# A depthwise convolution shared out between three engines: GpSimd takes one channel tile of eight, TensorE four instead of five

## What is computed

```python
def conformer_conv(h, n_seg, w_pw1, b_pw1, w_dw, b_dw, ln_g, ln_b, w_pw2, b_pw2):
    B, L, D = h.shape
    u = h @ w_pw1 + b_pw1
    a, gate = jnp.split(u, 2, axis=-1)
    u = a * jax.nn.sigmoid(gate)
    u = dwconv(u.reshape(B * n_seg, L // n_seg, D), w_dw).reshape(B, L, D) + b_dw
    u = jax.nn.silu(layer_norm(u, ln_g, ln_b))
    return u @ w_pw2 + b_pw2
```

## Time and profile before

| | |
|---|---|
| median of 3 runs | 2293.07 us (2291.17 to 2293.07) |
| span of the profiled execution | 2286.9 us |
| TensorE, matmuls | 2214.6 us busy, 97% of the span |
| VectorE | 985.8 us, 43% |
| ScalarE | 393.5 us, 17% |
| GpSimd | 67.6 us, 3% |
| chain that ended last, by engine | TensorE 66%, issue 22%, DMA 7%, VectorE 3%, ScalarE 1% |

### The profile page before, as it was taken

One profiled execution on the slowest core, in us unless ns is written; L12 is line 12 of the kernel. 1 busy time (PEld: TensorE's weight loads), 2 busy tenths in 40 slices (PEclk: granted clock), 3 DMA queues, 4 the chain that ended last, 5 costly groups with the idle time before them and its releaser, 6 DMA issues.

```text
span 2286.9 us, 24807 instructions
## 1 busy us (share of the span) xinstructions
PE 2214.6 (97%) x10134; PEld 1284.9 (56%) x10134; DVE 985.8 (43%) x1358; ACT 393.5 (17%) x748; POOL 67.6 (3%) x84
## 2 busy tenths in 40 slices
PE   7999999999999999999899999999999899999998
PEld 3343488888885556765544444445885544444443
DVE  2883297788845651861322222115541322222222
ACT  3214222012123210750200000002000200000000
POOL 1100100000020000001000000000000000000000
PEclk9999999999999999999899999999999899999999
DMA  9316244677541111021699999998211399999996
GB/s 349 144 42 232 99 147 147 227 260 279 190 166 46 37 37 68 22 107 69 249 423 428 428 429 428 429 428 326 74 74 74 143 424 429 428 429 428 430 428 275
DMA packets 106458, 564.55 MB, mean 247 GB/s; under 512 B 8584, under 2 KB 17422, under 8 KB 78734
## 3 DMA queue, kind: packets, MB, share of 16 engines
q1 hardware_dynamic: 105952, 563.35, 61.3%
q10 hardware_dynamic: 430, 0.13, 0.0%
HBM read 561.36 MB, written 2.10 MB: 246 GB/s over the span
## 4 chain that ended last, share of the span: by engine, by line
PE 66%; issue 22%; DMA 7%; DVE 3%; ACT 1%; POOL 0%; DVEq 0%; SPq 0%; ACTq 0%; POOLq 0%
PE psum L1503 20%; PE psum L1257 15%; PE psum L1926 8%; PE psum L1912 4%; DMA ring<-in_moe_w_down_dram 3%; PE psum L1698 3%; PE psum L2005 2%; PE psum L1819 2%; PE psum L1962 2%; DMA ring<-in_mlp_w_dram 2%; PE psum L1450 2%; PE psum L1750 1%; PE psum L1777 1%; PE psum L1399 1%; DMA ring<-in_moe_w_up_dram 1%
## 5 line engine op out<-in xcount | busy, mean ns | idle before, releaser
L1926 PE MATMUL psum<-ring,arena 128*64 128x512 f32 x2048 | 444.5, 593 | 4.9 <-DMA ring<-in_moe_w_up_dram 4.9
L1926 PEld LDWEIGHTS psum<-ring,arena 128*64 128x64 f32 x2048 | 145.0, 137 | 301.2 <-issue 287.6
L1257 PE MATMUL psum<-hT,ring 128*128 128x512 f32 x608 | 267.4, 597 | 3.8 <-ACT hT L852 3.8
L1912 PE MATMUL psum<-ring,arena 128*64 128x512 f32 x768 | 224.5, 594 | 1.9 <-DMA ring<-in_moe_w_down_dram 1.9
L2653 DVE TENSOR_TENSOR arena<-psum,arena 128x512 f32<-128x512 f32 x32 | 33.9, 1059 | 409.9 <-PE psum L1926 409.9
L1257 PEld LDWEIGHTS psum<-hT,ring 128*128 128x128 f32 x608 | 116.0, 192 | 150.1 <-issue 143.4
L1503 PE MATMUL psum<-ring 128*128 128x256 f32 x640 | 142.9, 380 | 3.7 <-DVE rstd L2358 3.7
L1503 PE MATMUL psum<-hT,ring 128*128 128x256 f32 x608 | 138.8, 385 | 0.8 <-ACT hT L846 0.8
L1503 PEld LDWEIGHTS psum<-ring 128*128 128x128 f32 x640 | 121.0, 190 | 23.5 <-issue 7.3
L1962 PEld LDWEIGHTS psum<-arena 128*128 128x128 f32 x1024 | 120.8, 198 | 14.0 <-issue 14.0
L1503 PEld LDWEIGHTS psum<-hT,ring 128*128 128x128 f32 x608 | 117.1, 193 | 18.4 <-issue 2.2
(11 more groups left out here) (349 smaller groups left out, 2480.4 us busy)
## 6 DMA issues: line engine op xcount, KB each, us to landing
ring<-in_moe_w_gate_dram SPq DMA_DIRECT2D x64, 2048.0 KB, 19.1
ring<-in_moe_w_up_dram SPq DMA_DIRECT2D x64, 2048.0 KB, 16.2
ring<-in_moe_w_down_dram SPq DMA_DIRECT2D x44, 2048.0 KB, 19.6
ring<-in_ada_w_dram SPq DMA_DIRECT2D x24, 2048.0 KB, 8.7
ring<-in_mlp_w_dram SPq DMA_DIRECT2D x16, 2048.0 KB, 8.5
hT<-in_moe_w_down_dram SPq DMA_DIRECT2D x16, 2048.0 KB, 14.2
ring<-in_w_mod_dram SPq DMA_DIRECT2D x12, 2048.0 KB, 12.9
ring<-in_conv_w_in_dram SPq DMA_DIRECT2D x6, 2048.0 KB, 19.3
```

Of the source, the lines that this page charges most:

```text
L1257: ins = pe.matmul(bank[:, 0:width], w[:, k, col:col + P], src(k), start=start and k == 0, stop=stop and k == kts - 1)
L1912: ins = pe.matmul(psum[64 * e:64 * e + 64, bank + nh, :], src[:, 4 * h + k, 64 * e:64 * e + 64], w[:, k, nh * N:(nh + 1) * N], start=h == ...
L1926: ins = pe.matmul(psum[64 * nh:64 * nh + 64, bank + e, :], src[:, 4 * h + k, 64 * e:64 * e + 64], w[:, k, nh * N:(nh + 1) * N], start=h == ...
```

## The change

GpSimd convolves channel tile 1. VectorE convolves tiles 0, 2 and 4, TensorE tiles 3, 5, 6 and 7. [...] Its padded input `upad_pool` lies in the place of a constant that is loaded later. It does this after the first two tap matrices and before the last two. The orders on TensorE and ScalarE are written out anew; the means are summed in the order 0, 2, 1, 3, 4, 5, 6, 7. There is a 13th tap transfer. VectorE waits for its previous own tile to be complete before it writes `upad` again.

```diff
-N_TAPS = 12
-PE_CONV = (0, 2, 4, 6, 7)
-DVE_CONV = (1, 3, 5)
+N_TAPS = 13
+PE_CONV = (3, 5, 6, 7)
+DVE_CONV = (0, 2, 4)
+POOL_CONV = (1,)
...
-        if j % 2:
-            T_CV[j - 1] = tiles(["act"])
-    T_CV[DT - 1] = tiles(["act"])
+        if j == 5:
+            T_CV[3] = tiles(["act"])
+    for j in (5, 6, 7):
+        T_CV[j] = tiles(["act"])
...
+        upad_pool = carve(K, KCOL["cos"][0], SEGS, UPAD)
+        tap_u = carve(rms, 0, SEGS, SEG)
...
-                for m, j in enumerate(DVE_CONV):
-                    dst = vec_rows[0:TAPS, 5, :] if m == 2 else vec_rows[48 + TAPS * m:48 + TAPS * (m + 1), 2, :]
+                for m, j in enumerate(DVE_CONV + POOL_CONV):
+                    dst = vec_rows[TAPS * (m - 2):TAPS * (m - 1), 5, :] if m >= 2 else vec_rows[48 + TAPS * m:48 + TAPS * (m + 1), 2, :]
                     rows(sp, dst, A["conv_w_dw"][0][:, j * P:(j + 1) * P], "taps_in")
...
-            for m, j in enumerate(PE_CONV):
+
+            def spread_taps(m):
+
+                j = PE_CONV[m]
                 if m >= 2:
                     pool.wait_ge(S["tile_done"], T_CV[PE_CONV[m - 2]] + 1)
...
+            def pool_conv(m):
+
+                j = POOL_CONV[m]
+                pool.wait_ge(*emptied(T_PW1[j])(1))
+                link(pool.tensor_tensor(upad_pool[:, :, PAD:PAD + SEG],
+                                        glu_a[:, j % 2, :].rearrange("p (s w) -> p s w", s=SEGS),
+                                        glu_s[:, j % 2, :].rearrange("p (s w) -> p s w", s=SEGS), ALU.mult))
+                acc = cv[:, j, :].rearrange("p (s w) -> p s w", s=SEGS)
+                for k in range(TAPS):
+                    at = COL[f"w_own{len(DVE_CONV) + m}"] + k
+                    w, u = vecT[:, at:at + 1], upad_pool[:, :, k:k + SEG]
+                    if k == 0:
+                        ins = pool.tensor_scalar(acc, u, w, vecT[:, COL["b_dw"] + j:COL["b_dw"] + j + 1], ALU.mult,
+                                                 ALU.add).then_inc(S["u_pool"], 1)
+                        pool.wait_ge(S["u_pool"], m + 1)
+                    else:
+                        link(pool.tensor_scalar(tap_u, u, w, None, ALU.mult))
+                        ins = pool.tensor_tensor(acc, acc, tap_u, ALU.add)
+                        if k < TAPS - 1:
+                            link(ins)
+                ins.then_inc(S["conv_pool"], 1)
+
+            link(pool.memset(upad_pool[:, :, 0:PAD], 0.0))
+            link(pool.memset(upad_pool[:, :, PAD + SEG:UPAD], 0.0))
+            spread_taps(0)
+            spread_taps(1)
+            pool_conv(0)
+            spread_taps(2)
+            spread_taps(3)
...
-            for m in range(4):
-                pw1(2 * m)
-                spread(m)
-                pw1(2 * m + 1)
-                conv_out(2 * m)
-                if m == 3:
-                    spread(4)
+            for j in range(5):
+                pw1(j)
+            spread(0)
+            pw1(5)
+            conv_out(3)
+            pw1(6)
+            spread(1)
+            spread(2)
+            pw1(7)
+            conv_out(5)
+            spread(3)
+            conv_out(6)
...
-            for m in range(4):
-                pw1(2 * m)
-                if m == 0:
-                    pe.wait_ge(S["taps_in"], 16 * N_TAPS)
-                    pe.wait_ge(S["tap_pad"], 1)
-                    turn_tile(T_TAPS, [(vec_rows[0:VEC_ROWS[g], g, :], VEC_ROWS[g]) for g in range(2, 6)])
-                if m == 2:
-                    pe.wait_ge(S["rms_ready"], 1)
-                if m >= 2:
-                    conv_mean(2 * m - 3)
-                pw1(2 * m + 1)
-                conv(2 * m)
-                if m == 3:
-                    mod_gemv(1)
-                if m:
-                    conv_mean(2 * m - 2)
+            pw1(0)
+            pe.wait_ge(S["taps_in"], 16 * N_TAPS)
+            pe.wait_ge(S["tap_pad"], 1)
+            turn_tile(T_TAPS, [(vec_rows[0:VEC_ROWS[g], g, :], VEC_ROWS[g]) for g in range(2, 6)])
+            pw1(1)
+            pw1(2)
+            pw1(3)
+            pe.wait_ge(S["rms_ready"], 1)
+            conv_mean(0)
+            pw1(4)
+            pw1(5)
+            conv_mean(2)
+            conv(3)
+            pw1(6)
+            pw1(7)
+            conv_mean(1)
+            conv(5)
+            conv_mean(3)
+            conv(6)
+            conv_mean(4)
+            mod_gemv(1)
             conv_mean(5)
             conv(7)
...
                 m = DVE_CONV.index(j)
+                if m:
+                    dve.wait_ge(S["conv_done"], m)
                 dve.wait_ge(*emptied(T_PW1[j])(1))
...
             for j in range(DT):
                 if j in PE_CONV:
                     glu(j)
-                else:
+                elif j in DVE_CONV:
                     own_conv(j)
```

More of the change, by code:

```diff
@@ L64 @@
     ("b_mod2", 48), ("w_own0", TAPS), ("w_own1", TAPS), ("to_next_block", 18),
-    ("w_dw", ROUNDS * 32), ("w_own2", TAPS),
+    ("w_dw", ROUNDS * 32), ("w_own2", TAPS), ("w_own3", TAPS),
 ):
@@ L68 @@
     _at += _w
-VEC_ROWS = [128, 123, 48 + 2 * TAPS, 128, 128, TAPS]
+VEC_ROWS = [128, 123, 48 + 2 * TAPS, 128, 128, 2 * TAPS]
 KCOL = {}
@@ L279, in block_kernel @@
         K = sb("K", [P, KW])
-        vecT = sb("vecT", [P, 5 * P + TAPS])
+        vecT = sb("vecT", [P, 5 * P + 2 * TAPS])
         cpad = sb("cpad", [P, DT, 32])
@@ L425, in block_kernel @@
             "n_ms", "n_inv", "n_wide", "half_scaled", "half_ready", "late_sq",
-            "u_base", "u_ready", "u_spread", "u_own", "conv_done", "mean_done", "mean_sb", "centered",
+            "u_base", "u_ready", "u_spread", "u_own", "u_pool", "conv_done", "conv_pool", "mean_done", "mean_sb", "centered",
             "x_pw2", "gains", "hid_ready", "mlp_wsum", "mlp_wsum4", "mlp_tsum", "mlp_part", "mlp_m1", "mlp_read",
@@ L885, in pw1 @@
                         act.wait_ge(S["u_ready"], PE_CONV.index(j - 2) + 1)
-                    elif j >= 2:
+                    elif j - 2 in DVE_CONV:
                         act.wait_ge(S["u_own"], DVE_CONV.index(j - 2) + 1)
+                    elif j - 2 in POOL_CONV:
+                        act.wait_ge(S["u_pool"], POOL_CONV.index(j - 2) + 1)
                     col = COL["b_pw1"] + (8 if m == 0 else 0) + j
@@ L1457, in conv_mean @@
                     pe.wait_ge(*emptied(T_CV[j])(0))
+                elif j in POOL_CONV:
+                    pe.wait_ge(S["conv_pool"], POOL_CONV.index(j) + 1)
                 else:
```

## The result

The changed kernel takes 2308.44 us (median of 4 runs, 2306.99 to 2311.59), the kernel before 2292.12 us (4 runs) beside it: +16.3 us, ratio 1.0082, 95% interval 1.0069 to 1.0096. The forecast was +26.3 us, in a range of +11 to +43. The profiled execution has a span of 2305.8 us, 18.9 us longer than before, and the stage accounts for it: TensorE begins the sums after the mean 17.95 us later.

What follows compares the result with a forecast made beforehand. TensorE was taken to bound the stage; +30.7 us (late) +2.6 (clock) -7.0 (removed convolution) = +26.3 us, on the profiled 2286.9 us and the 6.2 us to the median: 2319.4 us. Range +11 to +43 us.

Steps and rivals of the forecast that it cites:

- removed convolution: One of five tile convolutions on TensorE taken out of the stage: -7.0 us if nothing waits.
- Price of a sum to a step: Time a GpSimd sum adds to a linked VectorE step while GpSimd's tile runs: 0.95 us.
- Price of a tensor_scalar: Time a GpSimd tensor_scalar adds to a VectorE step: 0.50 us taken, between nothing or 0.36 and 0.95.
- The pace: While GpSimd's tile runs, each VectorE step loses 0.725 us; a multiply-add goes every 1.51 us instead of 0.787.
- three signs of being wrong: Multiply-adds at 0.8 us beside GpSimd, multiply-adds alternating 1.7 and 0.75, or a wait on GpSimd's own tile.
- Late by 30.7: TensorE starts tile 3's convolution at 156.7 us instead of 126.0, after waiting for VectorE's tile 2 and replicas: +30.7 us.
- The clock: After its wait TensorE runs at the lower clock, near 0.5 for 5 us: +2.6 us, between 0 and 2.6.
- forecast's own lower bound: Low end for the forecast's own case, +20 to +42 us, 2313 to 2335 us.
- rival A: GpSimd's tensor_scalar operations hold nobody on VectorE: 14 us fewer, +12, 2305 us; chance 0.12.
- rival B: Faster: VectorE's slack takes all the holding, so the 7.0 us show, 2286 us; chance 0.05.
- Rival C: GpSimd's tensor_scalar is dearer than its sum, 1.5 us with a hold of 1.3: 22 more, 2342 us; chance 0.10.
- Rival D: Looser turns, VectorE getting two steps in between now and then: a loss of 0 to 12 us; chance 0.05.

Runs made afterwards that it cites:

- run without taps: Changed kernel with GpSimd's 30 further taps of tile 1 left out, gate product and first tap kept (result not computed): 2283.69 us, 8.3 less than the kernel before.

## Why the prediction was right, and where it was off

- **TensorE carries the stage; its removed convolution is worth 7.0 us:** right, shown by the run without taps (7.85 us at the sums after the mean).
- **GpSimd's reads and VectorE's two-input steps exclude one another, in turns:** right, and shown by taking the reads away (multiply-adds back to 0.79 us) and by leaving one kind of operation at a time.
- **Price of a sum to a step:** 0.95 us forecast, 0.89 measured. **Price of a tensor_scalar:** 0.50 forecast, 0.31 measured, just under the lower bound of 0.36 that came from the memset row. A tap of GpSimd thus costs VectorE 1.20 us and not 1.45, some 7.5 us less over 30 taps. This is the term that made the sum too large.
- **The pace was wrong too.** I let each VectorE step meet an operation, 0.725 us on each, because I took a tensor_scalar as short (0.8 us). It takes 1.57 at the shortest and 1.88 here, so a third, free step fits into a tap: 1.2/3 = 0.40 us on each. Tile 2 therefore ended at 128.6 us, not 145.3, and convolution 3 started at 137.45, not 156.7. The run with the two-operation form (1.02 us) has a tensor_scalar nearly as short as I had assumed, and no free step. There tile 2 ends at 139.5 and convolution 3 starts at 149.7, 6 and 7 us before the forecast's, and the time is that of the changed kernel. So the pace decides where the waits fall; of the 10 us by which the forecast was too high some 7.5 are, by this estimate, the prices.
- **What followed was therefore also misplaced.** Some 58 operations were to be over by convolution 3; about 39 were. GpSimd ended at 178.4, not 163, so that its own mean was waited for, which was one of the three signs of being wrong that I had named, and VectorE's tile 4, which I had undisturbed, took 35.60 us. Late by 30.7 became late by 13 at convolution 3 (it started at 124.30 us in the run without taps), and 6.4 us of waiting that I had excluded came after it. The 1.5 us of waiting for tile 0's mean did not come.
- **The clock:** I gave it 2.6 us once. Four waits cost 7.1 us in all.
- **The sum:** +30.7 + 2.6 - 7.0 = +26.3 against +18.3 + 7.1 - 7.0 = +18.4 in the profiled stage, +16.3 in the medians. The total that VectorE loses was close: 57 x 0.725 = 41 us forecast, 36.3 measured against the run without taps, of it 28.8 in the multiply-adds (99.3 us busy against 70.5) and the rest in products, first taps and replicas. What a lost VectorE microsecond costs depends on where it falls, and that I had put too early.
- **How much of it was luck.** The sign and the size of the loss follow from turns that are there. But +16.3 lies below the +20 that I gave as the forecast's own lower bound; the stated range holds it only because it was drawn down to rival A. And the errors went both ways: too much waiting before convolution 3, and nothing for the waits and the slower clock that came behind it.
- **Rival A** (only sums hold, +12 us) is refuted by the 1.06 us steps, though its time was nearer to the measured one than the forecast's; **rival B** (VectorE's slack takes it) by the waits. **Rival C:** the tensor_scalar was indeed dearer than the sum for GpSimd, but not for VectorE, and the price to VectorE is what C's extra time rested on. **Rival D** (looser turns) had the free step, here one in every tap, but its loss of 0 to 12 us was too small. I gave it 0.05; it deserved more.

## What to carry to other kernels

Before giving elementwise work to GpSimd beside a VectorE that runs two-input steps, count what its reads take from VectorE: here 60 operations took 36 us from VectorE, where the whole tile on VectorE takes 25. Cost it in turns, one operation against one step, and with GpSimd's own lengths measured by form, since the length decides how early the loss falls. And where TensorE must wait for another engine, give it work whose inputs are there: here the wait of 5.16 us and the slow mean behind it both went.

## What the runs showed of the hardware

- A GpSimd tensor_scalar of 128x512 with one operation (times a per-partition scalar) took 1.57 us at the shortest and 1.88 beside VectorE; the same with a second operation (plus 0.0) took 1.02 beside VectorE. I had not expected more arithmetic to be faster. Why, no run here tells.
- GpSimd holds VectorE only for part of its operation: 0.31 of some 1.57 us, 0.89 of some 1.26 (a sum of that size at 250.18 us in the kernel before). The Trainium skill (SBUF — State Buffer, Who interferes with whom) says that the one that comes second blocks until the first has finished. The runs agree for who blocks whom, not for how long.
- Memsets on GpSimd, which read nothing, left two-input multiply-adds alone (23.59 us for 30) but held VectorE's one-input tensor_scalar: 0.98 against 0.55 us.
- After a wait of only 3.35 us TensorE's next matmuls ran at the lower clock (a mean of 2.07 us instead of 1.02). After one of 3.85 us (the run with the sums only) the mean still took 1.10 us and the clock fell behind it, to 0.50 from 101.4 to 104 us. After waits of 0.76 us (the tensor_scalars only) and 1.31 us (four tiles on VectorE) the convolution took its usual 7.07 us.
